# Reordering the top-k, rope, value-turning and gate steps of two sparse-attention layers

## The reference

```python
a, g, zc, q, k, v, za, qi, ki, wi = jnp.split(h @ w_in[l], IN_SPLITS, axis=-1)
y_conv = silu(layer_norm(depthwise_conv(a * sigmoid(g), 31 taps))) * silu(zc)
q, k, qi, ki = (apply_rope_2(t, cos, sin) for t in (q, k, qi, ki))
# per query: index scores, the 68 best keys (topk = 272 // 4), attention over them
logits = jnp.einsum('bqhd,bsd->bqhs', qi, ki) * IDX_SCALE
score = jnp.einsum('bqhs,bqh->bqs', jax.nn.relu(logits), wi * IDX_W_SCALE)
score = jnp.where(causal, score, -inf); idx = lax.top_k(score, topk)
s = jnp.where(valid, q . k[idx] * HEAD_DIM ** -0.5, -inf)     # 8 heads of 64
y_attn = (softmax(s) . v[idx]) * silu(za)
h = layer_norm(ALPHA * h + concat([y_conv, y_attn]) @ w_out[l])
```

## Time and profile before

| what | us |
|---|---|
| median of 3 runs | 963.73 |
| runs | 967.8, 961.78, 963.73 |
| the profiled execution | 961.15 |
| its span on the core | 959.3 |
| TensorE busy in the span | 884.5 |
| VectorE, ScalarE, GpSimd busy | 526.2, 470.6, 618.6 |

### The profile page before, as it was taken

The page is one execution under the profiler, slowest core; times in us unless marked ns, Lnnn a source line. Parts: engine busy times, 40 slices in busy tenths (PEclk is TensorE's granted clock), DMA queues, the critical chain, the costliest instruction groups (busy, mean ns, idle before and its releaser), DMA issues.

```text
span 959.3 us, 16864 instructions
## 1 busy us (share of the span) xinstructions
PE 884.5 (92%) x6758; PEld 842.9 (88%) x6758; DVE 526.2 (55%) x1095; ACT 470.6 (49%) x909; POOL 618.6 (64%) x360
## 2 busy tenths in 40 slices
PE   3999899999998998999999997999989889998985
PEld 2987599989997898999999997999888889997885
DVE  5213111189955826755331114988983659799655
ACT  3535555642346434643444444345558454544673
POOL 4521454545556898799998897866852877664051
PEclk9999999999999999899999998999979989998997
DMA  9522543443432355365555672754220527454001
GB/s 259 164 78 88 176 132 91 131 117 104 133 107 73 129 175 177 110 197 177 186 177 159 184 220 58 221 156 150 90 88 1 176 56 219 141 157 147 1 1 44
DMA packets 133991, 125.97 MB, mean 131 GB/s; under 512 B 6405, under 2 KB 131962, under 8 KB 133914
## 3 DMA queue, kind: packets, MB, share of 16 engines
q1 hardware_dynamic: 133360, 124.17, 42.1%
q10 hardware_dynamic: 554, 0.73, 0.2%
HBM read 123.70 MB, written 1.05 MB: 130 GB/s over the span
## 4 chain that ended last, share of the span: by engine, by line
PE 78%; DVE 9%; ACT 5%; POOL 4%; DMA 3%; issue 2%; SPq 0%; ACTq 0%; DVEq 0%
PE PS L577 21%; PE PS L579 20%; PE PS L578 20%; PE PS L813 3%; DMA ring<-in_w_in 3%; POOL w_lo L1068 2%; PE PS L568 2%; ACT w_hi L1190 1%; PE PS L962 1%; PE PS L934 1%; PE PS L991 1%; DVE zoneB L1910 1%; PE PS L779 1%; DVE zoneB L1632 1%; DVE PS L1855 1%
## 5 line engine op out<-in xcount | busy, mean ns | idle before, releaser
L1068 POOL TENSOR_TENSOR w_lo<-ring,w_hi 128x1024 fp32r<-128x1024 f32 (+1 forms) x235 | 540.2, 2313 | 267.1 <-ACT w_hi L1190 255.4
L577 PE MATMUL PS<-x_hi,w_hi 128*128 128x256 f32 (+2 forms) x1560 | 460.4, 295 | 23.9 <-POOL x_lo L1078 9.3
L579 PE MATMUL PS<-x_hi,w_lo 128*128 128x256 f32 (+2 forms) x1560 | 447.6, 287 | 0.0
L578 PE MATMUL PS<-x_lo,w_hi 128*128 128x256 f32 (+2 forms) x1560 | 446.6, 286 | 0.0
L577 PEld LDWEIGHTS PS<-x_hi,w_hi 128*128 128x128 f32 (+1 forms) x1560 | 297.7, 191 | 29.5 <-issue 26.1
L578 PEld LDWEIGHTS PS<-x_lo,w_hi 128*128 128x128 f32 (+1 forms) x1560 | 297.0, 190 | 1.6 <-issue 0.5
L579 PEld LDWEIGHTS PS<-x_hi,w_lo 128*128 128x128 f32 (+1 forms) x1560 | 297.2, 191 | 0.0
L1190 ACT ACTIVATE w_hi<-ring 128x1024 fp32r<-128x1024 f32 (+1 forms) x231 | 233.5, 1013 | 84.8 <-PE PS L579 79.1
L1173 ACT ACTIVATE zoneA<-PS 128x272 f32<-128x272 f32 (+4 forms) x80 | 31.7, 397 | 142.1 <-PE PS L579 141.1
L1855 DVE SCALAR_TENSOR_TENSOR PS<-zoneA,cols,PS 128x256 f32<-128x256 f32 x240 | 98.5, 480 | 0.1
L1173 ACT ACTIVATE zoneB<-PS 128x256 f32<-128x256 f32 (+4 forms) x115 | 40.9, 379 | 86.6 <-DVE PS L1822 39.4
(11 more groups left out here) (275 smaller groups left out, 1218.7 us busy)
## 6 DMA issues: line engine op xcount, KB each, us to landing
ring<-in_w_in SPq DMA_DIRECT2D x58, 1024.0 KB, 5.4
ring<-in_w_ffn_in SPq DMA_DIRECT2D x22, 1024.0 KB, 5.1
ring<-in_w_out SPq DMA_DIRECT2D x12, 1024.0 KB, 5.2
ring<-in_w_ffn_out SPq DMA_DIRECT2D x16, 704.0 KB, 4.7
ring<-in_w_mla_o SPq DMA_DIRECT2D x4, 1024.0 KB, 5.1
ring<-in_w_hg_o SPq DMA_DIRECT2D x4, 1024.0 KB, 5.1
ring<-in_w_kv_b SPq DMA_DIRECT2D x2, 1024.0 KB, 5.5
ring<-in_w_q_b SPq DMA_DIRECT2D x2, 768.0 KB, 4.5
```

What stands on the lines that cost most here:

```text
L577: mm(out_, hi_w, hi_x, start=start, stop=False)
L578: mm(out_, hi_w, lo_x, start=False, stop=False)
L579: return mm(out_, lo_w, hi_x, start=False, stop=stop)
L1068: sub(lo_w, src, hi_w, ALU.subtract).then_inc(sem("w_lo"), 1)
```

## The change

In both sparse layers:
- VectorE runs top-k rounds 0 and 1 before rope 0, and in general round i + 1 before rope i, for i = 0 to 6; then round 8; then `sel` of tile 0 alone. Rope 7 stands behind the mask of attention step 0, `sel` of tile 1 behind the mask of step 1. The 32 taps of steps 0 to 9 are dealt out as 2, 2, 5, 4, 4, 3, 3, 3, 3, 3.
- TensorE turns values beside the rope: one group each after rope 3, 4 and 5. ScalarE copies them there.
- Attention starts at five ropes done. Each even head's first scores wait for its own k tile, and the first two transposes wait for ropes 7 and 8 (they use the rope banks).
- The gate chunk za2 moves from attention step 9 to step 1.
- ScalarE loads the table of the exponent after the seventh chunk of the rope phase.
- In layer 0 GpSimd's four `first_taps` move from behind piece za1 to places before the pieces of k0, k2, v0 and v2.

```diff
--- before.py
+++ after.py
@@ -194,7 +194,6 @@
     return f"ffi{j // 2 * 2 + up}", j % 2
 
 
-Z_EARLY = 6
 IDX_FIRST = [("q", 0), ("q", 1)]
 IDX_FILL = [("q", 2), ("q", 3), ("k", 0), ("k", 1), ("k", 2), ("k", 3), ("v", 0), ("v", 1)]
 ROPE_FILL = [("v", 2), ("v", 3), ("zc", 0), ("zc", 1), ("zc", 2), ("zc", 3), ("za", 0), ("za", 1)]
@@ -205,9 +204,11 @@
 
 def z_chunks(l, s):
 
-    n = DSA_N[l] + DSA_LAG + 1
-    m = 8 - Z_EARLY
-    return [("zc" if z < 4 else "za", z % 4) for z in range(Z_EARLY + s * m // n, Z_EARLY + (s + 1) * m // n)]
+    return {1: [("za", 2)], DSA_N[l] + DSA_LAG: [("za", 3)]}.get(s, [])
+
+
+TAPS_AT_ATT = [0, 2, 4, 9, 13, 17, 20, 23, 26, 29, 32]
+TURN_AT = {3: 0, 4: 1, 5: 2}
 
 
 ORDER = [("start", 0)]
@@ -233,8 +234,9 @@
 for _l in range(DEPTH2):
     ORDER += [part(f"L{_l}{n}", 2 * j + i) for j in range(2) for n in ("g", "a") for i in range(2)]
     ORDER += [(f"L{_l}kw", 0), part(f"L{_l}qi", 0), (f"L{_l}kw", 1)]
-    ORDER += [part(f"L{_l}{n}", i) for n, i in [("qi", 1), ("qi", 2), ("qi", 3)] + IDX_FIRST + IDX_FILL + ROPE_FILL]
-    ORDER += [(f"L{_l}vt", i) for i in range(3)]
+    ORDER += [part(f"L{_l}{n}", i) for n, i in [("qi", 1), ("qi", 2), ("qi", 3)] + IDX_FIRST + IDX_FILL]
+    for _i, (_n, _m) in enumerate(ROPE_FILL):
+        ORDER += [part(f"L{_l}{_n}", _m)] + ([(f"L{_l}vt", TURN_AT[_i])] if _i in TURN_AT else [])
     ORDER += [part(f"L{_l}{n}", i) for s in range(DSA_N[_l] + DSA_LAG + 1) for n, i in z_chunks(_l, s)]
     ORDER += [part(f"L{_l}wo", c) for c in range(DC)]
 ORDER += [("out", i) for i in range(4)]
@@ -942,13 +944,14 @@
                         pe.wait_ge(sem("score"), 16 * (l + 1))
                     out_of_psum(pe, *part(f"{T}{'q' if i < 4 else 'k'}", i % 4))
                     rope("q", 8 * l + i, q2[:, i, q_from:L] if i < 4 else k2[:, i - 4, :], 4)
-                out_of_psum(pe, *part(f"{T}v", 3))
-                for x, (t0, n) in enumerate(KEY_CHUNKS):
-                    g = CHUNK[f"{T}vt", x]
-                    bank_free(g)
-                    for c in range(4):
-                        last = nc.tensor.transpose(PS[0:n, BANK[g], c * P:(c + 1) * P], vT2[:, c, t0:t0 + n], ident)
-                    done(last)
+                    if i in TURN_AT:
+                        t0, n = KEY_CHUNKS[TURN_AT[i]]
+                        g = CHUNK[f"{T}vt", TURN_AT[i]]
+                        bank_free(g)
+                        out_of_psum(pe, *part(f"{T}v", 3))
+                        for c in range(4):
+                            last = nc.tensor.transpose(PS[0:n, BANK[g], c * P:(c + 1) * P], vT2[:, c, t0:t0 + n], ident)
+                        done(last)
 
                 def dsa_attention(i):
 
@@ -958,6 +961,8 @@
                         if i >= 2:
                             pe.wait_ge(sem(f"{A}_masked"), i - 1)
                         b = PS[:, 2 + i % 2, 0:nk]
+                        if i < HEADS and h % 2 == 0:
+                            pe.wait_ge(sem("q_roped"), 8 * l + 5 + h // 2)
                         if i < DSA_TILES:
                             last = mm(b, q2r[:, h // 2, q0:q0 + P], k2r[:, h, 0:nk], start=True, stop=True)
                         else:
@@ -974,6 +979,8 @@
                             pe.wait_ge(sem("meta_p"), 1)
                         if j >= 2:
                             pe.wait_ge(sem(f"{A}_pt_out"), j - 1)
+                        else:
+                            pe.wait_ge(sem("q_roped"), 8 * l + 7 + j)
                         p, b = at2_p[:, j % (DSA_LAG + 1), :], PS[:, 4 + j % 2, :]
                         if j < DSA_TILES:
                             for k0 in range(0, width, P):
@@ -992,7 +999,7 @@
                                       v2[:, k0 // P, h * HD:(h + 1) * HD], start=(k0 == 0), stop=(k0 == width - P))
                         last.then_inc(sem(f"{A}_o"), 1)
 
-                pe.wait_ge(sem("q_roped"), 8 * (l + 1))
+                pe.wait_ge(sem("q_roped"), 8 * l + 5)
                 out_of_psum(pe, f"{T}vt", 2)
                 pe.wait_ge(sem("acc_out"), 2 * l + 1)
 
@@ -1148,10 +1155,10 @@
                     nc.gpsimd.memset(v2[:, 2, :], 0.0)
                 nc.gpsimd.memset(at2_p[:, :, META + P:2 * P], 0.0).then_inc(sem("pads"), 1)
                 if l == 0:
-                    lo_items(f"{T}g1", f"{T}za0")
-                    for c in range(CC):
+                    lo_items(f"{T}g1", f"{T}q1")
+                    for c, (first, last) in enumerate((("k0", "k0"), ("k1", "k1"), ("v0", "v0"), ("v1", "wo0"))):
                         first_taps(l, c)
-                    lo_items(f"{T}za1", f"{T}wo0")
+                        lo_items(f"{T}{first}", f"{T}{last}")
                 else:
                     lo_items(f"{T}g1", f"{T}wo0")
                 lo_piece(SPLIT[f"{T}wo1", 0])
@@ -1473,14 +1480,17 @@
                         take_acc(0)
                 for i, (n, m) in enumerate(ROPE_FILL):
                     take_proj(n, m)
+                    if i in TURN_AT:
+                        rows = KEY_CHUNKS[TURN_AT[i]][1]
+                        take(f"{T}vt", TURN_AT[i], v2[0:rows, TURN_AT[i], :], rows=rows, n=512)
+                    if i == 6:
+                        warm(ACT.Exp)
                     if i >= 4 and l == 0:
                         act.wait_ge(sem("q_roped"), i - 3)
                         for h in (2 * (i - 4), 2 * (i - 4) + 1):
                             r = slice(h % 2 * HD, h % 2 * HD + HD)
                             af(meta_q[r, h // 2, h * META:(h + 1) * META], q2r[r, h // 2, 0:META], ACT.Copy)\
                                 .then_inc(sem("meta_q"), 1)
-                for x, (t0, n) in enumerate(KEY_CHUNKS):
-                    take(f"{T}vt", x, v2[0:n, x, :], rows=n, n=512)
                 def dsa_attention(i):
 
                     A = f"{T}att"
@@ -1897,7 +1907,8 @@
                         at = TAPS_AT_IDX[s]
 
                 dve.wait_ge(sem("score"), 16 * (l + 1))
-                for r in range(ROUNDS):
+                def top_round(r):
+
                     for t in range(2):
                         nk = Q_TILES[t][2]
                         v.max(top8[:, t, :], score[:, t, 0:nk]).then_inc(sem("top"), 1)
@@ -1910,18 +1921,31 @@
                         v.match_replace(score[:, t, 0:nk], in_to_replace=top8[:, t, :], in_values=score[:, t, 0:nk],
                                         imm_value=NEG).then_inc(sem("top"), 1)
                     dve.wait_ge(sem("top"), 4 * (ROUNDS * l + r) + 4)
-                    if r < 8:
-                        m = r % 4
-                        out_of_psum(dve, *part(f"{T}{'q' if r < 4 else 'k'}", m))
-                        if r < 4:
-                            rope("q", 8 * l + r, q2[:, m, q_from:L], [q2r[:, m, q_from:L]], q_from, n_all, rope2_a, 4)
-                        else:
-                            rope("q", 8 * l + r, k2[:, m, :], [k2r[0:HD, 2 * m, :], k2r[HD:P, 2 * m + 1, :]],
-                                 0, L, rope2_a, 4)
-                for t in range(2):
+
+                def rope_qk(i):
+
+                    m = i % 4
+                    out_of_psum(dve, *part(f"{T}{'q' if i < 4 else 'k'}", m))
+                    if i < 4:
+                        rope("q", 8 * l + i, q2[:, m, q_from:L], [q2r[:, m, q_from:L]], q_from, n_all, rope2_a, 4)
+                    else:
+                        rope("q", 8 * l + i, k2[:, m, :], [k2r[0:HD, 2 * m, :], k2r[HD:P, 2 * m + 1, :]],
+                             0, L, rope2_a, 4)
+
+                top_round(0)
+                for i in range(7):
+                    top_round(i + 1)
+                    rope_qk(i)
+                assert ROUNDS == 9
+                top_round(8)
+
+                def allow(t):
+
                     q0, nq, nk = Q_TILES[t]
                     link(v.tensor_scalar(sel[:, t, 0:nk], score[:, t, 0:nk], NEG, NEG, ALU.not_equal, ALU.mult))
                     link(v.tensor_tensor(sel[:, t, 0:nk], sel[:, t, 0:nk], cst(CAUSAL[q0]), ALU.min))
+
+                allow(0)
 
                 def centre(tag, count, src, bank_):
 
@@ -1956,6 +1980,10 @@
                                                in1=sel[:, t, 0:nk] if s < DSA_TILES else cst("causal_m"),
                                                scale=-ATT_SCALE, scalar=BIG, op0=ALU.add, op1=ALU.min,
                                                accum_out=at2_min[:, s:s + 1]).then_inc(sem(f"{A}_masked"), 1)
+                    if s == 0:
+                        rope_qk(7)
+                    if s == 1:
+                        allow(1)
                     if s == DSA_N[0]:
                         dve.wait_ge(sem(f"{A}_exp"), DSA_N[l])
                         if l == 0:
@@ -1967,8 +1995,7 @@
                         dve.wait_ge(sem(f"{A}_exp"), s - DSA_LAG)
                         normed(s // HEADS - 1)
                     if s < CLN_STEP[l]:
```

(3 more changed lines are left out.)

## The result

| | before | after |
|---|---|---|
| median, 20 runs each (us) | 963.81 | 966.16 |
| range (us) | 960.86 to 967.8 | 964.2 to 969.55 |
| span of the profiled execution | 959.3 | 965.0 |

The ratio is 1.003, 95% interval 1.0019 to 1.0041: the change made the kernel slower by 1.8 to 4.0 us. The forecast was 960.8.

The account below looks back on a forecast made before the run. TensorE was taken as the bound, busy 884.5 of 959.3 us, with the column mean's start deciding. Gains of 1.6 us (layer 0) and 1.2 (layer 1), 2.9 together, took the median from 963.73 to 960.8, range 957.0 to 965.6.

Parts of the forecast that it names:

- part 1: Rope phase, a top-k round ahead: ropes paced by TensorE every 3.48 us, same place behind their matmuls, one more round done.
- the pattern: VectorE and GpSimd: cosine product L1632, both inputs in SBUF, takes 0.44 us free but 1.90 beside GpSimd's subtraction.
- Part 3: Layer 0's first taps earlier: TensorE waits 1.4 us for v2's piece (0 to 2.6); GpSimd without long debt at phase end.
- rival (b): TensorE's granted clock low at L1005 and L1011 without za2 at step 9: 965.0 in one layer, 969.2 in both; chance 0.08.
- Behind L1005 I find nothing changed: After the column mean's start, nothing was expected to change; L1005 forecast 1.6 us earlier in layer 0, 1.2 in layer 1.
- VectorE's debt from first mask to last tap: Attention: VectorE owes 15.18 us of masks and taps, rope 7 (1.83) and `sel` of tile 1 (0.8).
- The gain of layer 1: Layer 1's column mean L1005 starts at 896.94 instead of 898.18, 1.2 us earlier.
- The last rope matmuls: End of rope phase: layer 0's moves from 690.32 to 693.28 (1.4 + 1.56); layer 1's is 1.56 later.
- the wait for v2's weights: Layer 0's rope phase: v2's piece ready at 664.3, TensorE wants it at 662.93; a wait of 1.4 us charged.
- (a): Rope 7's L1632 loses to GpSimd's last subtraction: 963.0 in layer 1 alone, chance 0.18; 965.2 in both, 0.10.
- (c): More is gained: first taps cost no wait and the transposes hide, 5.1 us in all, 958.6; chance 0.14.
- (d): No effect: L1005 is late for another reason, such as ScalarE behind with exponents, 963.7; chance 0.08.

Follow-up runs that it names:

- e6: Changed kernel with the cosine table copied once per sparse layer into PSUM, read there by ropes 0 to 6; 962.41 us, ratio 1.0001.
- e7: Changed kernel with two first-tap groups early, two behind the last piece, and attention taps dealt evenly; 962.39 us, ratio 0.9995.
- e9: Changed kernel with only the 32 attention taps dealt evenly over steps 0 to 9 again; 965.78 us, ratio 1.0023.
- e18: e17 with the cosine table left in SBUF; 965.82 us, ratio 1.0029.
- e17: e15 with 13 more extra matmuls right ahead of the column mean's wait; 963.02 us, ratio 0.9998.
- e2: Changed kernel with gate chunk za2 back at attention step 9 in both layers; 968.75 us, ratio 1.0065.
- e3: Changed kernel with first taps back behind piece za1 and za2 back at step 9; 967.28 us, ratio 1.0049.
- e4: Kernel before with only layer 0's first-tap groups moved before k0, k2, v0 and v2; 964.05 us, ratio 1.0014.
- e11: e3 with attention taps dealt evenly and the cosine table in PSUM; 967.03 us, ratio 1.0037.
- e13: Changed kernel with cosine table in PSUM and extra, unused TensorE matmuls in attention steps 1 to 10; 962.64 us, ratio 0.9995.
- e15: e13 with 5 and 6 extra matmuls in steps 16 and 17, ahead of the last gate chunk; 962.79 us, ratio 0.9995.
- e10: Changed kernel with taps dealt evenly, cosine table in PSUM and za2 at step 7; 962.48 us, ratio 1.0001.

## Why the prediction was wrong

**The step that failed is part 1: "From there on the ropes are paced by TensorE ... So I forecast the ropes at the same place behind their matmuls".** It took a cosine product at its free 0.44 us. I had seen the pattern, named it ahead of part 1, and then priced it at rope 0 and rope 7 alone. Part 3 said "GpSimd then has no long debt at the end of the phase", which is right, and it didn't ask where the debt goes: to the start, seven subtractions under ropes 0 to 3, where they came one by one before. The products ended every 4.9 us, not every 3.48, the first mask of layer 0 came 2.9 us later than forecast for it, and the last tap 2.9 us later than before, past the 1.5 us that I had named as the sign of being wrong. Shown by e6, by e7 against e9 and by e18 against e17 (2.7, 2.8 and 2.8 us of the median), and by e2 against e3 (4.1 us at the last tap). The median missed the forecast by 2.35 + 2.9 = 5.3 us, so this step is about half of it.

**The second term is the clock, rival (b) in a form of its own.** I gave it 0.08, at the two means. In layer 0 it did hit L1012 (3.27 instead of 2.10) and what follows: from the start of the column mean to that of the squares' 7.94 us instead of 6.26, 1.68 us. In layer 1 it hit a place that I had called unchanged ("Behind L1005 I find nothing changed"): the last gate chunk and the transposes beside it, 1.94 us in the pair of profiles. How much of that belongs to the change isn't shown, since e4 has the fall with the old layer 1. My argument against the rival, that za2 fills step 1, looked at the wrong place: za2 was also what stood ahead of the mean. With it at step 9 (e2) TensorE stood still for 0.74 us ahead of layer 0's mean, which took 2.10 us; with it at step 1 for 1.76, and the mean took 3.27.

**What held.** VectorE's debt from first mask to last tap: forecast 15.18 + 1.83 + 0.8 = 17.81, measured 17.86 in both layers. The copy right behind the last tap: 0.03 us (L1442 at 717.40; the tap ends at 717.37). The gain of layer 1 at a full clock: 0.98 us in e18 for 1.2. Layer 1 up to the column mean, within 0.4 us everywhere. The last rope matmuls: +2.25 and +1.32 for +2.96 and +1.56; the wait for v2's weights was 0.70 instead of 1.4 (1.3 by its own terms, 664.24 - 662.93), so a term was half its size. With the cosine in PSUM layer 0 is as forecast too (column mean 2.08 us earlier for 1.6).

**The rivals.** (a) did not happen at rope 7 in the changed kernel (0.44 us at 699.74), but its mechanism is the one that cost the time, at ropes 0 to 6; e11 shows it at rope 7. (c) and (d) did not happen. The sum, from the two profiles: layer 0 +1.31 at the column mean and +1.68 of clock, layer 1 -1.58 and +1.94 of clock, 3.35 together, of 3.55 in the two layers' regions. The medians are 2.35 apart (1.8 to 4.0 by the ratio). By an estimate of mine, a profile of before with e4's fall in layer 1 would leave about 2 (3.55 less 1.52).

**What stays open.** In which of TensorE's gaps the clock falls. Over all 20 profiles, the column mean of either layer met a falling clock in none of the 30 cases with 1.15 us or less of idle TensorE ahead of it, and in eight of the ten with 1.67 to 2.15 us. That goes with the gap, but isn't settled by it: both cases without a fall are e13's, and e13 and e15 are the same up to the gap of layer 0. The 13 matmuls of e17 closed the gap, and the clock held there and fell later. In every kernel without extra matmuls it fell in each layer at least once. Whether a kernel that holds it throughout would measure the forecast 3 us wasn't shown; the best of the 18, e10 and e13 (0.8 and 0.6 us under the kernel before beside them), can't be told from it.

## What to carry to other kernels

Before moving a VectorE operation with both inputs in SBUF, or work on GpSimd, lay the two timelines over each other for every instance, not for the first and last: an operation that comes round on a beat can miss every gap. One operand in PSUM takes the problem away (here 2.7 us for one copy a layer). And a gain that only adds a wait to TensorE is worth less than it looks: check the granted clock in the next stretch in which TensorE sets the pace. In layer 0 of this kernel an earlier start of 1.58 us was given back in full by it (e2 against the changed kernel). And a difference of 2 us between two profiles of a kernel of 960 can be the place where the clock happened to fall: look for a part of the program that both kernels share, as layer 1 in e4.
